# One region for the sparse branch up to the choice, latent tiles in its background, and a delta rule begun beside the rows' tail

## What is computed

```python
def hybrid_token_mixer(...):          # first block: gated rows (mLSTM) and delta rule (RWKV)
    ...
    return jnp.concatenate([y_m, y_r], -1) @ w_out

def second_block(...):
    h = rms_norm(x, g_norm); proj = h @ w_in          # q_a k_a v_a q_i k_i w_i z_a c_q c_kv ...
    q_a = partial_rope(rms_norm(q_a, g_qn_a), cos_a, sin_a)      # 8 heads of 64
    k_a = partial_rope(rms_norm(k_a, g_kn_a), cos_a, sin_a)
    q_i, k_i = partial_rope(q_i, ...), partial_rope(k_i, ...)
    o_a = dsa_attention(q_a, k_a, v_a, q_i, k_i, w_i)
    #   index = sum_h relu(q_i . k_i) * w_i ; keep the top 128 keys of each query ; softmax over them
    q_b  = rms_norm(c_q, g_cq) @ w_uq                 # latent branch
    kv_b = rms_norm(c_kv, g_ckv) @ w_ukv
    ...
    merged = sum_n sigmoid(gate_n) * ((o_n * silu(z_n)) @ w_branch_n)
    x = x + merged @ w_out
```

## Time and profile before

| | us |
|---|---|
| three runs | 1928.23, 1931.80, 1931.84 (median 1931.8) |
| the profiled execution | 1929.16 |
| its span, first to last instruction | 1927.4 |
| TensorE busy | 1733.2 (90%) |
| VectorE, ScalarE, GpSimd busy | 885.3, 701.9, 727.8 |
| mean granted clock of TensorE | 0.945 |

### The profile page before, as it was taken

The page is one execution under the profiler, slowest core; times in us unless marked ns, Lnnn a source line. Parts: engine busy times, 40 slices in busy tenths (PEclk is TensorE's granted clock), DMA queues, the critical chain, the costliest instruction groups (busy, mean ns, idle before and its releaser), DMA issues. The chain is left out here.

```text
span 1927.4 us, 25419 instructions
## 1 busy us (share of the span) xinstructions
PE 1733.2 (90%) x10328; PEld 1304.2 (68%) x10328; DVE 885.3 (46%) x1462; ACT 701.9 (36%) x1182; POOL 727.8 (38%) x376
## 2 busy tenths in 40 slices
PE   6999968889998999999999987889787789987999
PEld 4866648768785878888788864644574456775777
DVE  5658774447523455333113807956212864313231
ACT  4334442233424432322233322224434255344431
POOL 5423323315540445555444535300323611452242
PEclk9999989989999999999999998969888889998999
DMA  4312110004330223322233420100212010432131
GB/s 168 129 55 60 61 35 24 3 15 147 115 98 22 88 77 102 96 91 94 88 99 98 135 78 22 50 16 6 71 53 73 11 44 12 131 115 72 60 104 55
DMA packets 39572, 138.56 MB, mean 72 GB/s; under 512 B 4384, under 2 KB 5664, under 8 KB 38304
## 3 DMA queue, kind: packets, MB, share of 16 engines
q1 hardware_dynamic: 39456, 136.93, 22.4%
HBM read 132.72 MB, written 4.19 MB: 71 GB/s over the span
## 5 line engine op out<-in xcount | busy, mean ns | idle before, releaser
L352 POOL TENSOR_TENSOR parts<-ring,parts 128x1024 fp32r<-128x1024 f32 (+3 forms) x251 | 571.6, 2281 | 946.6 <-ACT parts L343 946.2
L390 PE MATMUL banks<-h_hi,parts 128*128 128x512 f32 x1096 | 476.7, 435 | 31.2 <-ACT a_gate L570 9.8
L391 PE MATMUL banks<-h_lo,parts 128*128 128x512 f32 x1096 | 439.4, 401 | 0.0
L392 PE MATMUL banks<-h_hi,parts 128*128 128x512 f32 x1096 | 438.9, 400 | 0.0
L343 ACT CAST parts<-ring 128x1024 fp32r<-128x1024 f32 (+3 forms) x251 | 244.8, 979 | 234.2 <-PE banks L392 213.6
L390 PEld LDWEIGHTS banks<-h_hi,parts 128*128 128x128 f32 x1096 | 210.5, 192 | 113.3 <-issue 60.1
L391 PEld LDWEIGHTS banks<-h_lo,parts 128*128 128x128 f32 x1096 | 210.8, 192 | 57.8 <-issue 12.8
L392 PEld LDWEIGHTS banks<-h_hi,parts 128*128 128x128 f32 x1096 | 210.6, 192 | 49.9
L2617 ACT CAST ffn_act_hi<-ffn_gate 128x512 fp32r<-128x512 f32 x22 | 13.7, 621 | 167.1 <-DVE ffn_gate L2516 167.1
L2573 DVE TENSOR_TENSOR ffn_raw<-banks,ffn_root 128x512 f32<-128x512 f32 x22 | 15.2, 692 | 125.3 <-PE banks L392 125.2
L390 PE MATMUL banks<-ffn_act_hi,parts 128*128 128x512 f32 x176 | 69.8, 396 | 3.2 <-DVE ffn_gate L2516 3.2
(11 more groups left out here) (539 smaller groups left out, 3120.5 us busy)
## 6 DMA issues: line engine op xcount, KB each, us to landing
ring<-weights SPq DMA_DIRECT2D x211, 512.0 KB, 3.5
ring<-weights SPq DMA_DIRECT2D x24, 256.0 KB, 2.6
ring<-weights SPq DMA_DIRECT2D x8, 384.0 KB, 3.1
x<-xT SPq DMA_DIRECT2D x2, 1024.0 KB, 6.0
x<-xT SPq DMA_DIRECT2D x1, 2048.0 KB, 7.8
x_spill<-x SPq DMA_DIRECT2D x2, 1024.0 KB, 4.8
x<-x_spill SPq DMA_DIRECT2D x1, 2048.0 KB, 7.6
outT<-x SPq DMA_DIRECT2D x8, 256.0 KB, 2.0
```

The costliest lines, as they stand in the source:

```text
L352: self.nc.gpsimd.tensor_tensor(self.parts[:, t % PARTS, 1, 0:w], self.ring[:, t % SLOTS, 0:w], self.parts[:, t % PARTS, 0, 0:w].bitcast(F3 ...
L390: nc.tensor.matmul(out, w.hi, x.hi, start=first, stop=False)
L391: nc.tensor.matmul(out, w.hi, x.lo, start=False, stop=False)
L392: return nc.tensor.matmul(out, w.lo, x.hi, start=False, stop=last)
```

## The change

In the mixer, the fourth head's norm and the last weight tile stand between the steps of the delta rule's first group, in one stage: `rwkv_pairs` is now a set of functions (`rwkv_core`) that `mlstm` calls. The first lane uses other banks of PSUM in that group. VectorE's weighing of the last score comes before the third head's norm, and the load of `memT` moves to the end of this stage.

In the second block, `a_v`, the transposition, the norms, the rotation and the choice are one stage, `select_keys`. The index tiles are rotated first, the q and k tiles later, one in each of the first eight rounds of the choice. A rotation is now a product with sin and one with cos on VectorE and GpSimd, two matmuls into one bank, and a copy by ScalarE: one matmul more for each tile. The 32 steps of `a_v` stand between the eight late rotations. `CHOOSE_STEPS` is 36, and the background has the five tiles of `b_c` behind the gates: 17 tiles, 136 steps. `close_sparse` is one stage that projects `branch`, norms `b_c` beside it, and projects `b_uq`, `b_uk` and `b_uv`.

```diff
-CHOOSE_STEPS = 64
+CHOOSE_STEPS = 36
...
-            for n in range(MH * ST + 1):
+            for n in range(MH * ST):
...
+            fill.pe(pe, 4)
+            nums(pe, MH * ST - 1)
+            fill.pe(pe, 4)
+            spread_low(pe, MH - 1)
+
+            pe.wait_ge(*G("operands_made").ge(2))
+            pe.wait_ge(*G("values_made").ge(4))
+            core.pe_turn(pe, 0, 0, range(2))
+            pe.wait_ge(*fill.taken(LAST - 1))
+            core.pe_turn(pe, 0, 0, range(2, 3))
...
+            norm_sums(pe, MH - 1, 1)
+            last_pair.pe(pe, 2)
+
+            pe.wait_ge(*fill.taken(LAST))
+            core.pe_products(pe, 0, 0)
+            norm_sums(pe, MH - 1, 2)
+            core.pe_z(pe, 0, 0)
...
+            core.pe_rest(pe, 0)
+            core.pe_group(pe, 1)
...
+def select_keys(k, qk, qi, ki, wi, wiT, v, chosen, cos, sin, y, sg, gained_matrix, q_scale, background, fill):
...
+        def pe_rotate(pe, i):
+            x, m, c = items[i]
+
+            pe.wait_ge(*G("sin_taken").ge(i + 1))
+            if i >= 3:
+                pe.wait_ge(*G("rotated").ge(i - 2))
+            bank = k.banks[4 + i % 3]
+            nc.tensor.matmul(bank, m, by_sin[:, i % 2, :], start=True, stop=False)
+            pe.wait_ge(*G("cos_ready").ge(i + 1))
+            nc.tensor.matmul(bank, k.const("ident"), by_cos[:, i % 2, :], start=False, stop=True).then_inc(*G("swapped").inc())
...
+                for i in range(FIRST):
+                    pe_rotate(pe, i)
+
+                pe.wait_ge(*G("turned_taken").ge(1))
+                norms.pe_sums(pe)
+
+                pe.wait_ge(*G("rotated").ge(FIRST))
+                pe_dots(pe, 1)
+                norms.pe_means(pe)
+                pe_dots(pe, 2)
+                pe_dots(pe, 3)
+                norms.pe_turns(pe)
+
+                pe.wait_ge(*G("relu_ready").ge((ST - 1) * AH))
+                pe.wait_ge(*G("normed").ge(4))
+                for i in range(FIRST, len(items)):
+                    fill.pe(pe, 4)
+                    pe_rotate(pe, i)
                 background.pe(pe, CHOOSE_STEPS)
...
+                    if FIRST + r8 < len(items):
+                        if r8 == 0:
+
+                            dve.wait_ge(*G("normed").ge(4))
+                        dve_rotate(dve, FIRST + r8)
...
+def close_sparse(k, y, z, sg, merged, background, latent):
...
+    background.finish(gating)
...
+        def _(pe):
+            for m in range(DT):
+                freed(pe, m)
+                feature_major(yh, 4)(k, pe, first + m, bank(m))
+                if m == 2:
+
+                    pe.wait_ge(*G("squares_added").ge(3))
+                    for total, b in zip(totals, SUMS):
+                        nc.tensor.matmul(k.banks[b], k.const("ones"), total, start=True, stop=True).then_inc(*G("summed").inc())
+            for h in range(BH):
+                freed(pe, DT + h)
+                feature_major(ch, 3)(k, pe, uq + h, bank(DT + h), None if h else ready)
...
+            weigh(2)
+            recip(0)
+            weigh(3)
+            for i in range(3):
+                normed(i)
+            low(0)
+            weigh(4)
+            low(2)
+            weigh(5)
+            recip(1)
+            normed(3)
+            normed(4)
```

More of the change, by code:

```diff
@@ L11 @@
 import math
+from collections import namedtuple
 from contextlib import ExitStack, contextmanager
@@ new lines, in pe_lane_free, with pe_rest @@
+    def pe_lane_free(pe, g):
+        pe.wait_ge(*lanes[0].count("masked_ready").ge(4 * g + 4))
+        pe.wait_ge(*lanes[0].count("inv_ready").ge(n * g + 1))
+        pe.wait_ge(*lanes[0].count("z_taken").ge(g + 1))
+    def pe_rest(pe, g):
+        for other in lanes:
+            pe.wait_ge(*other.count("masked_ready").ge(4 * g + 4))
+            pe.wait_ge(*other.count("inv_ready").ge(n * g + 1))
+            pe.wait_ge(*other.count("z_taken").ge(g + 1))
+        for i in range(n):
+            for lane, own in groups[g]:
+                pe_cx(pe, g, lane, i)
+            for lane, own in groups[g]:
+                pe_xcx(pe, g, lane, i)
+        for lane, own in groups[g]:
+            pe_wu(pe, g, lane)
+            pe_parts(pe, g, lane)
@@ new lines, in pe_group, with act_rest @@
+    def pe_group(pe, g):
+        for other in lanes:
+            pe.wait_ge(*other.count("part_added").ge(2 * g))
+            pe.wait_ge(*other.count("part_copied").ge(2 * g))
+        for i in range(2):
+            if i:
+                pe_lane_free(pe, g)
+            pe_turn(pe, g, i, range(4))
+            pe_products(pe, g, i)
+            pe_z(pe, g, i)
+        pe_rest(pe, g)
+    def act_rest(act, g):
+        for i in range(n):
+            for lane, own in groups[g]:
+                act_cx(act, g, lane, i)
+        for lane, own in groups[g]:
+            act_wu(act, g, lane)
+            act_parts(act, g, lane, own)
@@ new lines, in act_group, with dve_rest, dve_group @@
+    def act_group(act, g):
+        for i in range(2):
+            act_turned(act, g, i, range(4))
+            act_z(act, g, i)
+        act_rest(act, g)
+    def dve_rest(dve, g):
+        for i in range(n):
+            for lane, own in groups[g]:
+                dve_level(dve, g, lane, i)
+        for lane, own in groups[g]:
+            dve_parts(dve, g, lane, own)
+    def dve_group(dve, g):
+        for i in range(2):
+            for step in range(3):
+                dve_masks(dve, g, i, step)
+        dve_rest(dve, g)
@@ L3045, in sparse_branch @@
+def sparse_branch(k, start, latent):
     nc = k.nc
```

700 lines of the change are left out of this document (445 added, 255 removed).

## The result

The changed kernel takes 1899.3 us (median of 4 runs, 1888.0 to 1900.2) against 1931.8: the ratio is 0.983, 95% interval 0.981 to 0.984. It is faster, by 32.5 us where 73.8 were forecast, and lies outside the range. The profiled executions differ by 29.0 us (span 1898.4 against 1927.4), and the forecast is settled against these.

The account below looks back on a forecast made before the run. TensorE, busy nine tenths of the span, was the bound, so only its waits and lower-clock time could be gained: 57.6 us in the second block plus 14 in the mixer, 1929.2 - 71.6 = 1857.6, say 1858; range 1843 to 1877.

Parts of the forecast that it names:

- I take 84.5: Sparse attention: 32 units with 32 steps take 84.5 us, as the latent attention did at mean clock 0.92.
- The forecast's second reason: Start of the sparse attention: the 4.28 us without a matmul ahead of it are gone, so TensorE isn't idle before it.
- Rival (b): Sparse attention: its first eight units again run at clock 0.50, 11.3 us lost, 1869; chance 0.14.
- The mixer: Delta rule's start: reordered work fills VectorE's waits, 14 us gained (range 9 to 17.5).
- The selection region: From its first matmul: choice begins at 44.5 us, TensorE ends last at 112.6 us, VectorE 10 us earlier.
- Rival (a): Choice: each sine product waits out a GpSimd instruction, eight cost 23 us instead of 9.3; 1863; chance 0.10.
- Finish and closing region: After the sparse attention: 68 steps take 47.9 us with the gating beside them, then the closing region takes 54.5.
- rival (d): Closing region: the latent norms' chain finishes later than TensorE's branch work, 12 us lost, 1870; chance 0.07.
- and its end, 1: Closing region: 1 us allowed for the region's end, within its 54.5 us.

Follow-up runs that it names:

- e10_all3: Changed kernel with the background bank evicted before the wait for the maximum, cos product before the split, and 40 background steps in the selection region: 1851.6 us.
- experiment 4: Changed kernel with the closing region's last weight-tile split moved to the region of the latent rotation: 1889.7 us.
- experiment 2: Changed kernel with no background step in the sparse attention (32 before); they run in the finish instead: 1872.6 us.

## Why the prediction was wrong

**The step that failed** is the attention: "I take 84.5", from the latent branch's attention, "the same code with 32 units and 32 steps". It is the same code, but its score matmuls contract 96 rows and those of the sparse attention 64 (the form `64*128` stands in the earlier trace rows). With 128 rows the sparse attention takes 86.4 us, with 64 the latent one takes 114.0. Two things make up the 33.9 us that were missing, both from the rows of this case:

- At the same clock a head takes 1.38 us longer with 64 rows: 11.0 us.
- The low time is 61.6 us instead of 13.5. What it costs can be read against `e10_all3`, which runs the same matmuls at clock 1.00: 118.4 - 84.5 is 33.9, of which 8.3 - 2.7 = 5.6 are waits, so 28.3 us for 61.6 us of low time, 0.46 of it. For the 48.1 us of difference that is 22.1 us (an estimate).

With 0.9 us of longer waits (8.3 against four of 1.85) this is 34.0 us. The forecast's second reason, that the idle 4.28 us ahead of the attention would be gone, was right and of no use: the clock was still up at 1227.05, and fell at the first bank wait inside.

**Rival (b)** named the right mechanism, the lower clock, in the wrong place and at half its size. It took the old first stretch, 32.4 us at 0.50, as something that happens once at the start, and priced it at 11.3 us. In fact it came behind every change of the bank inside, and cost 22 us more than was allowed for. The rows of before could have warned of it: 32 steps change the bank four times where 19 did twice, behind waits of 2.98 and 2.97 us. The longer heads stood in no rival.

**The mixer** was right: 14 forecast, 15.1 measured alone, 11.8 in the changed kernel. The levels begin at 291.69 (forecast 293), though the first one still runs at half clock. Of the waits that I counted, VectorE's for the norm's sums are 1.44 and 1.09 us, and TensorE's for the first lane's inverse is 2.41.

**The selection region** was right up to the choice: its rounds start 44.3 us behind its first matmul, forecast 44.5. From there on it took 5.0 us more than forecast (74.6 against 69.6), and TensorE's three waits for GpSimd's late cos products are 5.5: I had costed GpSimd's work, but not that a split which waits for ScalarE stands in its queue ahead of the product. Rival (a), VectorE held up by GpSimd, happened to one of the eight sine products, and to the sum ahead of the norm parts (VectorE's timeline):

```profile
1146.98 2.85 DVE L3129 TENSOR_TENSOR a_chosen<-a_chosen,consts 128x512 f32<-128x512 f32 x1
...
1166.08 2.71 DVE L3081 TENSOR_TENSOR a_y<-x,sin_a 128x512 f32<-128x512 f32 x1
```

The sine product began 0.2 us into a GpSimd split of 2.36 us and took 2.0 us more than its like (0.68). This bears out the mechanism, and the Trainium skill (SBUF — State Buffer, SBUF: two separate sides) has it as an exclusive lock of the port pair; but VectorE's rounds ended 14 us before TensorE, so these 2.0 were hidden; the sum's 2 us stand ahead of the first round and were not.

**Finish and closing region**: TensorE's last product ends at 1444.8, 99.3 us after the attention, 2.1 less than forecast without the end. The norms are hidden and TensorE doesn't wait for the third `b_uq` tile; rival (d) did not happen. What I had too small is "and its end, 1": the region ends with a split of the next tile, whose slot only the last product frees, so ScalarE's cast and GpSimd's split follow TensorE's end and the next region starts 4.8 us behind it (experiment 4).

## What to carry over

When a duration is taken from another stage of the same code, compare the shapes of its matmuls too: here 64 rows instead of 96 made every head longer at the full clock (11 us in all) and turned short dips of the clock into long ones (some 22 us). Work put behind waits of two microseconds on TensorE is not free even where TensorE has slack, because here such waits were followed by half the clock; empty the bank before the engine that empties it takes up its next wait. And look at what an engine's queue has ahead of the instruction that others wait for (the split before the cos product) and at what a region does after its last matmul.

## What was unexpected of the hardware

How soon the granted clock came back from its lower level (1.2 GHz) went with how many rows the matmuls of that stretch contract, at the same count of instructions and columns: some 15 us with 64 rows in the score matmuls, 3.3 with 128, and in the latent attention 57 us in all with 64 against 13.5 with 96. TensorE had no gap in those stretches. The same number of matmuls also took longer with 64 rows at the upper clock, 9.90 us a head against 8.52 with 128 and 8.53 with 96; why, and whether this is also what held the clock down, is open.

And 2 us of waiting were enough for it to fall: the Trainium skill (TensorE: Matmul & The Clock Gate, A second HAM failure mode: psum-queue depth-cycling) describes short waits between groups of matmuls that make the clock swing to and fro, with the way up paid each time. The trace agrees, with 61.6 us low behind four waits of 1.99 to 2.34 us and none behind the bank waits of 0.83 us. The length of the wait alone doesn't decide: a wait of 1.91 us in unit 0 with 40 steps brought nothing, and one of 1.73 us did; in the attention without steps (experiment 2), three of seven waits of 0.71 us did. What else decides was not settled.
